# One projection of a hybrid diffusion step: half products after Strassen in ten of fourteen weight blocks

## The reference

```python
def _trunk_layer(x, cond, p, layer_idx, ctx_k, ctx_v, s0):
    h = _rmsnorm(x, p['norm_g'][0]) * (1.0 + sc1) + sh1
    z = jnp.einsum('bld,de->ble', h, p['w_in'].astype(F32))
    hq, hff, hfb, hi, hg, aq, ak, av, hy = _split_cols(z)
    o_hg, s_fin = _hgrn_mixer(hq, hff, hfb, hi, hg, p['lb'], s0, p['hgrn_norm_g'])
    ...
    o_hy = _hyena_mixer(hy, filt_f, p['hy_skip'], p['hy_conv_w'], p['hy_conv_b'])
    mix = jnp.concatenate([o_hg, o_da, o_hy], axis=-1) @ p['w_out'].astype(F32)
    x = x + g1 * mix
    ...
```

## Time and profile before

| | us |
|---|---|
| median of three runs (4063.61 to 4067.07) | 4064.61 |
| span of the profiled execution, first to last instruction | 4062.0 |
| the stage of layer 0, 128.6 to 683.1 of the span | 554.5 |
| its stretch before the first transposes of keys | 136.9 |
| from there to the first level score | 55.8 |
| levels and outputs (321.3 to 519.6) | 198.3 |
| behind them, up to the first product of the next stage | 163.5 |

### The profile page before, as it was taken

How to read it: one execution, slowest core, us unless ns; L and a number is a source line. 1 busy time by engine, 2 the same in 40 slices (tenths; PEclk the granted TensorE clock), 3 DMA queues, 4 the chain that set the end, 5 groups by cost and what they waited for, 6 DMA issues and landing times. The chain is left out here.

```text
span 4062.0 us, 55619 instructions
## 1 busy us (share of the span) xinstructions
PE 3765.9 (93%) x23486; PEld 3026.0 (74%) x23486; DVE 1600.4 (39%) x2836; ACT 1160.4 (29%) x2938; POOL 216.9 (5%) x136
## 2 busy tenths in 40 slices
PE   8999998998959999999899999989989599999996
PEld 3577875667439999999735688656664499999995
DVE  4248723879251111111152577248783411111112
ACT  3442212874121111111145222138721211111112
POOL 2100001000000000000020000110000000000000
PEclk9999999998979999999999999999989799999998
DMA  9311022003247777777482111210122477777774
GB/s 332 110 43 48 30 81 84 1 1 122 90 161 265 270 274 270 273 278 279 166 322 73 49 45 40 78 74 1 56 73 95 176 279 276 270 272 279 278 279 168
DMA packets 318943, 645.84 MB, mean 159 GB/s; under 512 B 20126, under 2 KB 57630, under 8 KB 317928
## 3 DMA queue, kind: packets, MB, share of 16 engines
q1 hardware_dynamic: 305736, 595.09, 40.5%
q0 software_dynamic: 9216, 33.56, 3.5%
q10 hardware_dynamic: 3744, 13.63, 0.8%
HBM read 580.36 MB, written 61.88 MB: 158 GB/s over the span
## 5 line engine op out<-in xcount | busy, mean ns | idle before, releaser
L2232 PE MATMUL ps<-arena 128*128 128x144 f32 x8192 | 1017.0, 287 | 6.6 <-DVE arena L2450 6.6
L2232 PEld LDWEIGHTS ps<-arena 128*128 128x128 f32 x8192 | 1010.1, 191 | 14.6 <-DVE arena L2450 14.6
L292 PE MATMUL ps<-arena 128*128 128x384 f32 x1920 | 630.1, 489 | 7.3 <-PEq L89 7.3
L292 PEld LDWEIGHTS ps<-arena 128*128 128x128 f32 x1920 | 364.9, 191 | 256.3 <-issue 12.7
L2256 PE MATMUL ps<-arena 128*128 128x144 f32 x4096 | 507.1, 286 | 0.0
L2256 PEld LDWEIGHTS ps<-arena 128*128 128x128 f32 x4096 | 503.6, 190 | 0.0
L2461 DVE TENSOR_TENSOR arena<-arena,ps 128x144 f32<-128x144 f32 x256 | 77.8, 304 | 922.2 <-ACT arena L2338 922.2
L2338 ACT ACTIVATE arena<-ps 128x144 f32<-128x144 f32 x256 | 74.5, 291 | 988.3 <-PE ps L2232 988.3
L434 ACT ACTIVATE arena<-ps 128x384 f32<-128x384 f32 (+1 forms) x192 | 86.3, 449 | 677.5 <-PE ps L292 455.0
L2450 DVE TENSOR_SCALAR arena<-ps,mod 128x128 f32<-128x128 f32 x248 | 84.5, 403 | 448.4 <-PE ps L2210 448.4
L289 PE MATMUL ps<-arena 128*128 128x256 f32 x1152 | 255.4, 379 | 0.0
(11 more groups left out here) (347 smaller groups left out, 3520.5 us busy)
## 6 DMA issues: line engine op xcount, KB each, us to landing
arena<-in_w_gate SPq DMA_DIRECT2D x64, 2048.0 KB, 8.0
arena<-in_w_up SPq DMA_DIRECT2D x64, 2048.0 KB, 14.1
arena<-in_w_down SPq DMA_DIRECT2D x64, 2048.0 KB, 12.4
arena<-in_w_mod SPq DMA_DIRECT2D x24, 2048.0 KB, 13.8
arena<-in_w_in SPq DMA_DIRECT2D x28, 1024.0 KB, 5.1
arena<-in_dft_units SPq DMA_DIRECT2D x26, 512.0 KB, 9.4
arena<-x_rows SPq DMA_DIRECT2D x22, 512.0 KB, 6.4
filter_spectra<-arena SPq DMA_DIRECT2D x32, 256.0 KB
```

Of the source, the lines that this page charges most:

```text
L292: last = nc.tensor.matmul(m.ps[:, at:at + TC], m.Wr[:, slot % 2, k, jj * P:(jj + 1) * P], m.hT[:, k, q * TC:(q + 1) * TC], start=(k == 0), ...
L2232: last = nc.tensor.matmul(m.ps[:, at:at + CAP], m.wbuf[:, 2 * h + which, k, q * P:(q + 1) * P], m.xe[:, e % 2, k, :], start=(k == 0), stop ...
```

## The change

Ten blocks, the `FAST` ones, are computed by a form of Strassen's scheme. The 1024 by 256 weight block is seen as two by two parts of 512 by 128 (`a11`, `a12`, `a21`, `a22`) and the 1024 by 1152 tokens as two by two parts of 512 by 576 (`b11` to `b22`). Seven products of such parts (`STEPS`), instead of eight, give the block. Each step is done in two halves `c` of `CH` = 288 token columns, four products of 288 columns each.

Sums on the way in: GpSimd makes four sums of weight parts for each block (`forms`), VectorE four sums of token parts once for each layer (`t1` to `t4`), at the start of the stage. The four token sums are stored to DRAM (`forms_dram`) at the start, since the recurrence needs their place, and loaded again behind the levels (`m.h_again`) for the last five blocks.

Sums on the way out: steps 2, 4 and 6 add onto step 0's accumulator bank, step 5 onto step 3's. ACT copies the banks after steps 0, 2, 3 and 6 (`copies`) to the four quarters of the output, and VectorE adds the banks after steps 1, 4 and 5 onto quarters that ACT wrote (`adds`). `copied` and `added` count them, and TensorE waits for them before it writes on in the bank.

The order changes too. Blocks 1, 2, 0, 11 and 12 come first, 35 steps without a token piece between them; then the transposes with nine pieces of block 3, the state updates, five pieces, and the levels with a piece after 22 of 32, all of them token pieces of 256 columns. Behind the levels stand the blocks 5, 6, 7, 8 and 13. The transposes of cached keys and of the recurrence's output lie between steps, and the rotary work of a block lies beside the next one.

```diff
@@ -46,6 +46,8 @@
 EPS = 1e-6
 LEVELS = [64, 32, 16, 8, 4, 2, 1]
 TC = 384
+HT = TOK // 2
+CH = HT // 2
...
-W_ORDER = [1, 2, 0, 3, 11, 12, 13, 9, 10, 4, 5, 6, 7, 8]
+W_ORDER = [1, 2, 0, 11, 12, 3, 9, 10, 4, 5, 6, 7, 8, 13]
 TOK_BLOCKS = (3, 4, 9, 10)
+FAST = [b for b in W_ORDER if b not in TOK_BLOCKS]
+EARLY = 5
+STEPS = 7
 
...
@@ -155,10 +167,54 @@
...
+    with_piece = [n for n in range(NS) if n % 3 != 2]
+    assert len(with_piece) == len(TOK_PIECES) - BEFORE_LEVELS
+
+    KH = KD // 2
+    b11, b12 = m.hT[:, 0:KH, 0:HT], m.hT[:, 0:KH, HT:TOK]
...
+    def copied(u, step, c=1):
+        return 8 * u + COPIES[step] + c + 1
+
+    def added(u, step, c=1):
+        return 6 * u + ADDS[step] + c + 1
...
@@ -187,35 +243,28 @@
...
+            for n in range(4):
+                sp.wait_ge(s["t_made"], n + 1)
+                sp.dma_start(m.forms_dram[n], m.h_forms[n].rearrange("p k t -> p (k t)")).then_inc(s["t_stored"], 16)
...
@@ -225,9 +274,25 @@
...
+                if b >= 11:
+                    sp.wait_ge(s["copied"], copied(FAST.index(b), 6))
+                    i = (b - 11) * 2 + 1
+                    sp.dma_start(m.zhy_dram[i * P:(i + 1) * P, :], m.zstage[:, 1]).then_inc(s["hy_stored1"], 16)
+                if b == 12:
+                    sp.dma_start(m.mask[:, :, :, :], m.d["hg_mask"]).then_inc(s["mask_loaded"], 16)
+                    sp.wait_ge(s["s_cleared"], 1)
...
+                    for n in (1, 0, 2, 3):
+                        sp.dma_start(m.h_again[n], m.forms_dram[n].rearrange("p (k t) -> p k t", t=HT))\
+                            .then_inc(s[f"t_loaded{n + 1}"], 16)
...
+            for i in range(2):
+                sp.wait_ge(s[f"hy_stored{i}"], 48)
...
         def _(pool):
+            formed = Count(s["formed"])
+
+            def forms(u):
+
+                a11, a12, a21, a22 = w_parts(u)
+                s1, s2, s3, s4 = m.w_forms
+                w_loaded(pool, W_ORDER.index(FAST[u]))
+                if u == EARLY:
+                    pool.wait_ge(s["placed"], NS)
+                elif u:
+                    pool.wait_ge(s["done"], made(FAST[u - 1], 3))
+                formed.then_wait(pool, nc.gpsimd.tensor_tensor(s1, a21, a22, ALU.add))
+                formed.then_wait(pool, nc.gpsimd.tensor_tensor(s2, s1, a11, ALU.subtract))
+                if u == EARLY:
+                    for n in range(4):
+                        pool.wait_ge(s[f"av_stored{n}"], 16 * ((2 * NT - n + 3) // 4))
+                elif u:
+                    pool.wait_ge(s["done"], made(FAST[u - 1], 4))
+                formed.done(nc.gpsimd.tensor_tensor(s3, a11, a21, ALU.subtract))
+                if u and u != EARLY:
+                    pool.wait_ge(s["done"], made(FAST[u - 1], 5))
+                formed.done(nc.gpsimd.tensor_tensor(s4, a12, s2, ALU.subtract))
...
+            for u in range(EARLY):
+                forms(u)
+            pool.wait_ge(s["done"], made(FAST[EARLY - 1]))
+            pool.wait_ge(s["t_stored"], 64)
...
+            def products(u, step):
+
+                a11, a12, _, a22 = w_parts(u)
+                s1, s2, s3, s4 = m.w_forms
+                t1, t2, t3, t4 = m.h_forms if u < EARLY else m.h_again
+                w, h = [(a11, b11), (a12, b21), (s2, t2), (s1, t1), (s3, t3), (s4, b22), (a22, t4)][step]
+                if step == 0:
+                    w_loaded(pe, W_ORDER.index(FAST[u]))
+                    if u == EARLY:
+                        pe.wait_ge(s["out_taken"], 6)
+                if step in (2, 3, 4, 5):
+                    pe.wait_ge(s["formed"], 4 * u + {2: 2, 3: 1, 4: 3, 5: 4}[step])
+                if step in (2, 3, 4, 6):
+                    n = {2: 2, 3: 1, 4: 3, 6: 4}[step]
+                    if u == 0:
+                        pe.wait_ge(s["t_made"], n)
+                    elif u == EARLY:
+                        pe.wait_ge(s[f"t_loaded{n}"], 16)
+                for c in range(2):
+                    if step == 0 and u >= 2:
+                        pe.wait_ge(s["copied"], copied(u - 2, 6, c))
+                    elif step == 1 and u:
+                        pe.wait_ge(s["added"], added(u - 1, 1, c))
+                    elif step == 2:
+                        pe.wait_ge(s["copied"], copied(u, 0, c))
+                    elif step == 3 and u == EARLY:
+                        pe.wait_ge(s["taken"], len(TOK_PIECES))
+                    elif step == 3 and u:
+                        pe.wait_ge(s["added"], added(u - 1, 5, c))
+                    elif step == 4:
+                        pe.wait_ge(s["copied"], copied(u, 2, c))
+                    elif step == 5:
+                        pe.wait_ge(s["copied"], copied(u, 3, c))
+                    elif step == 6:
+                        pe.wait_ge(s["added"], added(u, 4, c))
+                    at = second_bank(c) if step == 1 else third_bank(c) if step in (3, 5) else first_bank(u, c)
+                    for k in range(KH):
+                        last = nc.tensor.matmul(m.ps[:, at:at + CH], w[:, k, :], h[:, k, c * CH:(c + 1) * CH],
+                                                start=(k == 0 and step in (0, 1, 3)), stop=(k == KH - 1),
+                                                skip_group_check=True)
+                    last.then_inc(s["done"], 1)
 
...
@@ -356,14 +493,18 @@
...
+            for u in range(EARLY):
+                for step in range(STEPS):
+                    products(u, step)
+            pe.wait_ge(s["copied"], copied(EARLY - 1, 6))
+            pe.wait_ge(s["added"], added(EARLY - 1, 5))
             for i in range(4):
                 turn_keys(i)
-                piece()
-            piece()
+                if i:
+                    for _ in range(NT // 3):
+                        piece()
             state_updates()
-            for _ in range(3):
+            for _ in range(BEFORE_LEVELS - NT):
...
+            for u in range(EARLY, len(FAST)):
+                if u == EARLY + 2:
                     pe.wait_ge(s["k_taken"], 2)
...
+                for step in range(STEPS):
+                    products(u, step)
+                    if (u, step) == (EARLY + 1, 2):
+                        turn_cached()
+                    if (u, step) == (end_u, 3):
+                        turn_recurrent()
+                    if (u, step) == (end_u, 5):
+                        turn_context()
...
+            def copies(u, step):
+
+                jj, half = {0: (0, 0), 2: (0, 1), 3: (1, 1), 6: (1, 0)}[step]
...
+                for ch in range(2):
+                    act.wait_ge(s["done"], made(b, step, ch))
+                    at = third_bank(ch) if step == 3 else first_bank(u, ch)
+                    nc.scalar.activation(product_out(u, jj, half, ch), m.ps[:, at:at + CH], ACT.Copy,
+                                         scale=product_scale(u)).then_inc(s["copied"], 1)
...
+            for step in (2, 3, 6):
+                copies(0, step)
+            for u in (1, 2):
+                copies(u, 0)
+                softplus(2 * u - 2, "softplus_x")
+                copies(u, 2)
+                copies(u, 3)
+                softplus(2 * u - 1, "softplus_x")
+                if u == 1:
+                    copies(u, 6)
...
+            copies(2, 6)
+            copies(3, 0)
...
+            copies(3, 2)
+            copies(3, 3)
...
+            copies(3, 6)
+            for step in (0, 2, 3):
+                copies(4, step)
...
+                    copies(4, 6)
...
+            copies(EARLY, 0)
...
+            act.wait_ge(s["taken"], len(TOK_PIECES))
+            nc.scalar.activation(m.gate[:, :, :], m.gate[:, :, :], ACT.Silu).then_inc(s["gate_shaped"], 1)
+            for step in (2, 3, 6):
+                copies(EARLY, step)
+            for u in range(EARLY + 1, len(FAST)):
+                for step in (0, 2, 3):
+                    copies(u, step)
...
+            t = Count(s["t_made"])
+            t1, t2, t3, t4 = m.h_forms
+            t.then_wait(dve, nc.vector.tensor_tensor(t1, b12, b11, ALU.subtract))
+            t.then_wait(dve, nc.vector.tensor_tensor(t2, b22, t1, ALU.subtract))
+            t.done(nc.vector.tensor_tensor(t3, b22, b12, ALU.subtract))
+            t.done(nc.vector.tensor_tensor(t4, b21, t2, ALU.subtract))
+
+            def adds(u, step):
+
+                jj, half, kept = {1: (0, 0, 0), 4: (1, 1, 3), 5: (0, 1, 2)}[step]
+                for ch in range(2):
+                    dve.wait_ge(s["done"], made(FAST[u], step, ch))
+                    dve.wait_ge(s["copied"], copied(u, kept, ch))
+                    at = second_bank(ch) if step == 1 else third_bank(ch) if step == 5 else first_bank(u, ch)
+                    out = product_out(u, jj, half, ch)
+                    nc.vector.scalar_tensor_tensor(out, m.ps[:, at:at + CH], product_scale(u), out, ALU.mult, ALU.add)\
+                        .then_inc(s["added"], 1)
...
-            for i in range(4):
+            adds(0, 4)
+            adds(0, 5)
...
```

(25 more changed lines are left out.)

333 lines of the change are left out of this document (177 added, 156 removed).

## The result

| | before | after |
|---|---|---|
| median, us | 4064.11 (4062.53 to 4067.07, 4 runs) | 4028.24 (4020.96 to 4030.42, 4 runs) |
| span of the profiled execution | 4062.0 | 4027.9 |
| stage of layer 0 | 554.5 | 534.1 |
| stage of layer 1 | 554.5 | 539.7 |

The ratio is 0.991, with a 95% interval of 0.9896 to 0.9924. The changed kernel is faster by 36 us, 35.1 of them in the two stages. The forecast was 58.6 us, and the measured time lies 4 us above its range (3996 to 4024).

What follows compares the result with a forecast made beforehand. TensorE was taken to bound the kernel, VectorE's chain the levels. Terms +4.0, +6.5, -22.8, -18.2 gave -30.5 us a layer, -61.0 for both; hand-offs at 1.2 a layer left -58.6: 4006 us, range 3996 to 4024.

Steps and rivals of the forecast that it cites:

- Products: Strassen blocks: a record of 288 columns takes 243 ns; ten blocks 272 us against 309.6, -37.6 us a layer.
- rival 3: Products don't shrink: a group's start costs a weight load now hidden, 27 us a layer, 4050 to 4065; chance 0.04.
- Hand-offs within blocks: Steps waiting for ACT's copies or VectorE's sums: zero cost taken; 1 to 2 us per block where cover is missing.
- Stage start: First block: token forms, sums and small chain let ACT's step 2 copy end at 16.5, wanted at 18.1; zero cost.
- rival 1: Late hand-offs: VectorE and GpSimd slow each other at stage start and rotary steps, 3 to 9 us a layer; chance 0.27.
- End of block five: Before the first transposes: gate chain and copy end at 29.5 against 27.2, +2.4 us; second transpose waits 0.7 more.
- To the levels: From first transposes to first score: 62.3 us against 55.8, +6.5, with an idle piece of 4.5.
- The levels: Levels and outputs: VectorE sets the pace, 175.5 us against 198.3, -22.8 a layer.
- a fall costs under 2 us, mostly under VectorE's chain: TensorE's clock falling behind idle pieces, about 4 us in fine levels, 4.5 before them; bounds 0 to 3 us a layer.
- from there a score, a piece, a plain score (9.6): End of the levels' first half, from the 14th operands: 9.6 us, then placing, span, operands, placing 8.7; 18.3 together.
- Behind the levels: Last five blocks, transposes and stage end: 145.3 us against 163.5, -18.2 a layer.
- rival 4: TensorE's clock falls for long in the levels, making the kernel slower, up to 4308 us; chance 0.03.

Runs made afterwards that it cites:

- experiment C: Against the changed kernel: fifteen token pieces before the levels instead of fourteen, the piece after the 20th score removed; 4022.66 us, ratio 0.9901.
- E alone: Against the changed kernel: sixteen token pieces before the levels, ten in each half, none ahead of the last scores; 3998.85 us, ratio 0.9842; repeated, 4003.92 us.

## Why the prediction was wrong

**Products: right.** In layer 0, from the end of the wait for ACT to the end of block five, 496 records take 120.3 us without the drain of the last, 242.6 ns each, against 243. Weight loads stayed hidden (192 ns, rival 3 falls).

**Hand-offs within blocks: right behind the first block.** Behind the levels TensorE was idle 0.5 us ahead of the five blocks, and waited for no copy and no sum in them.

**Stage start: wrong, by 1.4 and 3.9 us of waiting.** Step 4 of the first block was named as the place to look, with 1.6 us to spare. This was the condition of rival 1: the forms took 14.3 us instead of 10.4. The rival's price of 3.0 for each layer came out as 1.4 and 3.9, since in layer 1 two operations of the small chain also took 1.30 and 1.24 us beside GpSimd.

"Nothing in the rows shows an operation of VectorE stretched beside GpSimd" was true, but it looked at one engine only. The trace of the kernel before has both engines on two SBUF operands at once, and there it is GpSimd, the later one, that is longer. Of the next lines the first two are the rotary step, and the third is GpSimd at the same width without such an operation of VectorE beside it:

```profile
568.40 1.23 DVE L745 TENSOR_TENSOR arena<-arena 128x1024 f32<-128x1024 f32 x1
568.52 3.31 POOL L272 TENSOR_TENSOR arena<-arena 128x1024 f32<-128x1024 f32 x1 [265.18 <-DVE arena L743]
...
1155.86 2.34 POOL L2133 TENSOR_TENSOR arena<-arena 128x1024 f32<-128x1024 f32 x1 [474.88 <-DMA arena<-in_x]
```

The 0.97 us between 3.31 and 2.34 spoke for rival 1, and the forecast passed over it.

The second place of rival 1, the rotary steps, did happen on VectorE (the additions of L977 took 2.70 us in the mean beside GpSimd's sums and multiplications; the same ones took 1.23 before). It cost nothing: TensorE waited for no sum there. The forecast had 1.4 us to spare for them, and they took more: in the first such block they ended at 565.14, 19.7 us behind the start of that block (by 112 records of 243 ns from 518.27) where the forecast had 18. What covered it was another thing, the order of the steps: TensorE asks for the sum behind them only at step 6.

**End of block five: nearly right.** 1.76 and 0.93 us of waiting against 2.4 and 0.7.

**To the levels: right in layer 0** (62.9 against 62.3; an idle piece of 4.55 against 4.5), and 1.6 more in layer 1, where the clock fell once more, for 3.4 us, at the transposes.

**The levels: the step that failed.** The sum 62.7 + 18.3 + 8.1 + 2.2 + 59.1 + 17.6 + 7.5 = 175.5 is 9.2 short in layer 0:

- The first half took 86.1 and not 81.0. Of the 5.1, 2.7 stand before the end of the 14th operands, behind the slow first score. The step "a fall costs under 2 us, mostly under VectorE's chain" failed in both parts: the first score feeds VectorE's chain directly, nothing covers it, and experiment C gave 2.4 to 2.8.
- The other 2.4 are the end: 20.8 us (398.94 to 419.70) against 18.3. The step "from there a score, a piece, a plain score (9.6)" let the score begin at the operands' end. It began 2.2 us later (401.13 against 398.94), since TensorE was inside a piece. The sum followed VectorE's chain and took TensorE as free whenever VectorE asked.
- The second half took 82.2 and not 78.9: 1.9 in its end (19.5 against 17.6, the same mechanism) and some 1.4 in its start, where TensorE idled 3.86 us for VectorE and the clock was at 0.50 for 3.4 us behind that. With the clock up and other places of the pieces (E alone) that start is 0.9 us shorter; how much of it is the clock's, no run shows.
- The outputs took 8.26 and 8.15 us against 8.1 and 7.5.

The working compared loads over the whole half (12.95 us of TensorE work in 14.5 of three levels) and found VectorE the pace. That holds for the middle. In the last levels VectorE's step has no span and then no operands, while TensorE's has a double score, and there TensorE is the pace. Even my 18.3 held avoidable waiting: with the ends free it is 16.1 (E alone, from 397.17 to 413.23).

**Behind the levels: right**, 144.6 and 144.8 against 145.3.

**Clock: rival 4 did not come**; the mean in the halves was 0.97 and 0.98. But the bound of 3 us a layer was too low for layer 1: 2.8 at the first score and 1.6 at the transposes, beside what the start lost. The forecast read the clock from two idle pieces by their length, and the runs show shorter ones with a fall behind them (the last section).

All together 18.8 us of the miss are the levels; 5.4 the first stretch, 4.4 of it in layer 1; 2.8 the second; 1.2 came back behind the levels and 2.4 was the allowance for hand-offs. That makes 23.4 of the 24.5. The last 1.1 us lie outside the two stages.

## What to carry to other kernels

Where two engines hand work to each other, the one that is fuller on average does not set the pace everywhere: go through the first and the last steps one by one, with both queues side by side, and put filler work where the other engine's step is longest. The placing of thirty-six filler pieces, twenty of them left in the levels instead of twenty-two, was worth 24 us in the two stages here, where the whole change was worth 35. And the medians of one kernel, taken at different times, can differ by nearly the size of a 7 us effect: run both kernels side by side, and compare the profiled stages that the change touches.

## What the runs showed of the hardware

A GpSimd sum of 128 by 512 took 1.26 us alone and 3.46 to 3.58 beside a VectorE operation with two SBUF inputs, and that operation 3.5 to 3.7 instead of 2.56. A sum of 128 by 1024 on GpSimd took 2.34 us alone and 3.31 beside one of VectorE. Both engines show the wait as a longer instruction and not as idle time, so a table of busy shares hides it. Even a VectorE operation of 4 columns took 1.30 us beside GpSimd, and 0.23 without it.

Idle pieces of TensorE of 4.55 and 3.86 us in the changed kernel were followed by a stretch at 1.2 GHz; one of 3.7 us before the change and one of 1.09 us in experiment C were not. Their length alone does not tell it. The clock was at 0.51 behind an idle piece of 1.92 us in the run with a piece before the transposes and behind one of 2.46 us in C, and at the transposes of the changed kernel the same two idle pieces, 1.76 and 0.93 us, were followed by 1.00 in layer 0 and by 0.50 in layer 1. Where the clock was low at the first score it cost 2.4 to 2.8 us. In the run with a piece before the transposes it fell at 221 us of the stage, and the first half was 78.1 us against the 77.8 without a fall.
